# Second attention of a two-block transformer kernel: scores from stacked q_hi over q_lo in 128 array rows, weighted sum inside the gate unit

## The reference, cut to what matters

```python
q = rope(q_flat..., t); ks = rope(ks, t); kw = rope(kw, t)          # scaled by 64**-0.5
k_cmp = rope(compress_blocks(kc, ...), pos_c); v_cmp = compress_blocks(vc, ...)
p_cmp = masked_softmax(q @ k_cmp.T, pos_c <= t);  o_cmp = p_cmp @ v_cmp
p_sel = masked_softmax(q @ ks.T, causal);         o_sel = p_sel @ vs
p_win = masked_softmax(q @ kw.T, causal);         o_win = p_win @ vw
o = g[0] * o_cmp + g[1] * o_sel + g[2] * o_win    # g = sigmoid(gate_logits)
```

## Time and profile before

| | us |
|---|---|
| three timed runs | 1312.44, 1313.99, 1314.47; median 1313.99 |
| the profiled execution: its own time | 1314.33 |
| its span (first to last instruction) | 1312.3 |
| mean granted TensorE clock | 0.982 |
| PE busy | 1262.8 (96%) |
| DVE, ACT, POOL busy | 813.4, 589.7, 62.7 |

### The profile page before, as it was taken

One profiled execution on the slowest core, in us unless ns is written; L12 is line 12 of the kernel. 1 busy time (PEld: TensorE's weight loads), 2 busy tenths in 40 slices (PEclk: granted clock), 3 DMA queues, 4 the chain that ended last, 5 costly groups with the idle time before them and its releaser, 6 DMA issues.

```text
span 1312.3 us, 22759 instructions
## 1 busy us (share of the span) xinstructions
PE 1262.8 (96%) x8692; PEld 1138.8 (87%) x8692; DVE 813.4 (62%) x1294; ACT 589.7 (45%) x885; POOL 62.7 (5%) x72
## 2 busy tenths in 40 slices
PE   5899999999999999999998999998999999999997
PEld 3688888888886899889998999998898889999997
DVE  2677777753344755776675555655767767565664
ACT  2443234321233337544445556545445565544542
POOL 1000000000001000000001000002013102000001
PEclk9899999999999999999998999998899999999999
DMA  9544544453234244323453554544442224455542
GB/s 390 232 192 191 193 181 178 178 196 136 88 104 161 98 159 160 128 97 129 161 192 105 221 206 174 192 170 151 166 157 97 97 97 176 151 192 191 188 167 89
DMA packets 30957, 214.16 MB, mean 163 GB/s; under 512 B 3376, under 2 KB 4656, under 8 KB 5936
## 3 DMA queue, kind: packets, MB, share of 16 engines
q1 hardware_dynamic: 30032, 209.73, 43.4%
q10 hardware_dynamic: 864, 3.58, 0.7%
HBM read 212.24 MB, written 1.05 MB: 163 GB/s over the span
## 4 chain that ended last, share of the span: by engine, by line
PE 87%; DVE 5%; ACT 3%; DMA 3%; issue 1%; DVEq 0%; ACTq 0%; SPq 0%
PE ps_u L1510 26%; PE ps_u L1511 26%; PE ps_u L1512 26%; DMA raw<-in_stream 1%; PE ps_a L1457 1%; DMA scr<-in_mods 1%; PE ps_a L1446 1%; DVE w_lo L848 1%; ACT w_hi L486 1%; PE ps_a L1474 1%; DVE sq L925 1%; PE ps_a L1663 1%; PE ps_a L1648 1%; PE ps_a L1823 1%; PE ps_a L1463 1%
## 5 line engine op out<-in xcount | busy, mean ns | idle before, releaser
L1510 PE MATMUL ps_u<-x_hi,w_hi 128*128 128x256 f32 (+1 forms) x1744 | 544.3, 312 | 14.8 <-DVE x_lo L936 10.3
L1511 PE MATMUL ps_u<-x_lo,w_hi 128*128 128x256 f32 (+1 forms) x1744 | 537.8, 308 | 0.0
L1512 PE MATMUL ps_u<-x_hi,w_lo 128*128 128x256 f32 (+1 forms) x1744 | 537.4, 308 | 0.0
L848 DVE TENSOR_TENSOR w_lo<-raw,w_hi 128x1024 fp32r<-128x1024 f32 x322 | 393.9, 1227 | 210.7 <-ACT w_hi L486 209.0
L486 ACT ACTIVATE w_hi<-raw 128x1024 fp32r<-128x1024 f32 x322 | 338.2, 1056 | 285.1 <-PE ps_u L1512 247.1
L1510 PEld LDWEIGHTS ps_u<-x_hi,w_hi 128*128 128x128 f32 x1744 | 336.2, 193 | 39.6 <-issue 20.5
L1511 PEld LDWEIGHTS ps_u<-x_lo,w_hi 128*128 128x128 f32 x1744 | 336.5, 193 | 15.4 <-issue 0.5
L1512 PEld LDWEIGHTS ps_u<-x_hi,w_lo 128*128 128x128 f32 x1744 | 336.2, 193 | 15.2
L1510 PE MATMUL ps_u<-h_hi,w_hi 128*128 128x256 f32 (+1 forms) x800 | 246.0, 308 | 1.4 <-DVE h_lo L1426 1.4
L1511 PE MATMUL ps_u<-h_lo,w_hi 128*128 128x256 f32 (+1 forms) x800 | 245.1, 306 | 0.0
L1512 PE MATMUL ps_u<-h_hi,w_lo 128*128 128x256 f32 (+1 forms) x800 | 245.0, 306 | 0.0
(11 more groups left out here) (237 smaller groups left out, 823.0 us busy)
## 6 DMA issues: line engine op xcount, KB each, us to landing
raw<-in_stream SPq DMA_DIRECT2D x153, 1024.0 KB, 4.7
wide_scr<-in_mods SPq DMA_DIRECT2D x18, 1024.0 KB, 6.8
scr<-in_mods SPq DMA_DIRECT2D x18, 1024.0 KB, 7.2
raw<-in_stream SPq DMA_DIRECT2D x8, 768.0 KB, 4.1
x<-in_tokens ACTq DMA_DIRECT2D x2, 1024.0 KB, 14.1
wide_scr<-in_cmp_w SPq DMA_DIRECT2D x2, 1024.0 KB, 9.1
sq<-in_cmp_w SPq DMA_DIRECT2D x2, 1024.0 KB, 7.8
out<-x SPq DMA_DIRECT2D x4, 256.0 KB, 2.2
```

The costliest lines, as they stand in the source:

```text
L848: dve.tensor_tensor(w_lo[:, k % 2, cols], raw[:, k % 2, cols], w_hi[:, k % 2, cols].bitcast(F32), ALU.subtract).then_inc(l_ready, 1)
L1510: pe.matmul(dst, wh, xh, start=(kc == 0), stop=False)
L1511: pe.matmul(dst, wh, xl, start=False, stop=False)
L1512: ins = pe.matmul(dst, wl, xh, start=False, stop=(kc == span - 1))
```

## The change

The scores no longer use plain fp32 matmuls over 64 rows. ACT makes an fp32r copy of each rotated operand and DVE the rest (value minus copy). For the queries the copy lies in one half of the 128 partitions and the rest in the other (`q2_st`, in the unused half of `x_hi`); for the keys the copy lies in both halves (part 0) and the rest over the first half with zeros opposite (part 1; `k2_st` in `x_lo`, `kc_st` in `h_hi`). A score is then two fp32r matmuls over 128 rows. POOL no longer copies queries, and `pool_group(r)` no longer waits for scores. `weighted(h-1)` computes 128 output rows (both groups; one is read) and stands before the last two of the eight row blocks of gate unit h. PE's heads are written out, not looped.

```diff
+        q2_st = x_hi[:, :, S:NB]
+        kc_st = h_hi[:, 4, 0:2 * G2 * NCP].rearrange("p (a g c) -> p a g c", a=2, g=G2)
+        k2_st = x_lo[:, :, S:NB].rearrange("p (a g b) n -> p a g b n", a=2, g=G2)
 # POOL
             for r in range(4):
-                pool.wait_ge(rope2_done, 3 + r if r < 2 else 4 + r)
-                if r:
-                    pool.wait_ge(qk_done, HQ + 2 * r)
-                else:
-                    pool.wait_ge(hid_turned, 1)
+                if r == 0:
+                    pool.wait_ge(hid_done, 2)
                     pool.wait_ge(gt_ready, 1)
-                pool.tensor_copy(q_cur[:, 0, :], q2[:, r, :]).then_inc(qcur_ready, 1)
                 pool_group(r)
 # ACT
+            def keys_hi():
+                act.wait_ge(rope2_done, 2)
+                for g in range(G2):
+                    for half in range(2):
+                        act.activation(k2_st[half * DH:(half + 1) * DH, 0, g, :, :],
+                                       kk2[g * DH:(g + 1) * DH, :].rearrange("p (b n) -> p b n", b=2), ACT.Copy).then_inc(k2_hi, 1)
+            def cmp_keys_hi():
+                act.wait_ge(k2_zeroed, 1)
+                act.wait_ge(rope2_done, 5)
+                for g in range(G2):
+                    for half in range(2):
+                        act.activation(kc_st[half * DH:(half + 1) * DH, 0, g, 0:NC], kc_r[g * DH:(g + 1) * DH, 1, :], ACT.Copy)\
+                           .then_inc(k2_hi, 1)
+            def queries_hi(r):
+                act.wait_ge(rope2_done, 3 + r if r < 2 else 4 + r)
+                for g in range(G2):
+                    rows = slice(g * DH, (g + 1) * DH)
+                    act.activation(q2_st[rows, 2 * r + g, :], q2[rows, r, :], ACT.Copy).then_inc(q2_hi, 1)
...
+            keys_hi()
             splits(0, k + 7)
+            queries_hi(0)
+            cmp_keys_hi()
+            queries_hi(1)
             splits(0, k + 8)
...
             head(0, 0, 0, None, first=True)
+            for r in range(2, R2H):
+                queries_hi(r)
 # DVE: keys_lo(), cmp_keys_lo() wait for all of k2_hi of their kind, two subtractions each
+            def queries_lo(r):
+                dve.wait_ge(q2_hi, G2 * (r + 1))
+                for g in range(G2):
+                    rows, others = slice(g * DH, (g + 1) * DH), slice((1 - g) * DH, (2 - g) * DH)
+                    dve.tensor_tensor(q2_st[others, 2 * r + g, :], q2[rows, r, :], q2_st[rows, 2 * r + g, :].bitcast(F32), ALU.subtract)\
+                       .then_inc(q2_stacked, 1)
...
             queries(1)
+            for g in range(G2):
+                dve.memset(k2_st[(1 - g) * DH:(2 - g) * DH, 1, g, :, :].bitcast(F32), 0.0)
+            dve.memset(kc_st.bitcast(F32), 0.0).then_inc(k2_zeroed, 1)
+            keys_lo()
...
             rope2(4, kc_r[:, 0, :], ps_a[:, 1, 0:NC], cos2[:, last:S:CS], sin2[:, last:S:CS], kc_r[:, 1, :])
+            queries_lo(0)
+            cmp_keys_lo()
+            queries_lo(1)
             pool_in(1)
...
             head(0, 0, 0, None, first=True)
+            for r in range(2, R2H):
+                queries_lo(r)
 # PE
+            def scores(h, g, first=False):
+                pe.wait_ge(q2_stacked, h + 1)
+                if first:
+                    pe.wait_ge(k2_stacked, 2 * G2)
+                else:
                     pe.wait_ge(exp_done, 2 * HQ + h)
...
+                for a in range(2):
+                    pe.matmul(lo, q[0], k2_st[:, a, g, :, 0:P], start=(a == 0), stop=(a == 1))
                 for qt in range(TT):
+                    for a in range(2):
+                        pe.matmul(ps_a[:, 1, 2 * P + qt * 16:2 * P + qt * 16 + 16], q[qt], kc_st[:, a, g, :],
+                                  start=(a == 0), stop=(a == 1))
+                for a in range(2):
+                    ins = pe.matmul(hi, q[1], k2_st[:, a, g, :, :], start=(a == 0), stop=(a == 1))
+                ins.then_inc(qk_done, 1)
...
-                    pe.matmul(ps_a[rows, 2, 0:S], v2_tok[:, b, 0, rows], probs_t[:, 2 * b, :], start=(b == 0), stop=False)
+                    pe.matmul(ps_a[:, 2, 0:S], v2_tok[:, b, 0, :], probs_t[:, 2 * b, :], start=(b == 0), stop=False)
...
-                unit(r, FIRST["gates2"] + g, from_x(S))
-                weighted(h - 1, 1 - g)
+                def weighted_within(kc):
+                    if kc == KD - 2:
+                        weighted(h - 1)
+                unit(0, FIRST["gates2"] + h, from_x(S), ready=weighted_within)
```

More of the change, by code:

```diff
@@ L312, in program @@
         rope2_done = sem("rope2_done")
+        k2_zeroed = sem("k2_lo_zeroed")
+        k2_hi = sem("k2_hi_done")
+        k2_stacked = sem("k2_stacked")
+        q2_hi = sem("q2_hi_done")
+        q2_stacked = sem("q2_stacked")
         v2_turned = sem("v2_turned")
@@ L1785, in _ @@
             pe.wait_ge(rope2_done, 5)
[L1788 to L1792, removed]
-                    pe.wait_ge(exp_done, 2 * HQ + h)
-                q = [q_cur[rows, 0, qt * P:(qt + 1) * P] for qt in range(TT)]
-                own = kk2[rows, :].rearrange("p (b n) -> p b n", b=2)[:, :, 0:P]
-                pe.matmul(ps_a[:, 1, 0:2 * P].rearrange("p (b n) -> p b n", b=2), q[0], own, start=True, stop=True)
-                for qt in range(TT):
-                    pe.matmul(ps_a[:, 1, 2 * P + qt * 16:2 * P + qt * 16 + NC], q[qt], kc_r[rows, 1, :], start=True, stop=True)
-                pe.matmul(ps_a[:, 0, :], q[1], kk2[rows, :], start=True, stop=True).then_inc(qk_done, 1)
+            def scores(h, g, first=False):
[3 more added lines that the diff above has]
+                else:
+                    pe.wait_ge(exp_done, 2 * HQ + h)
+                q = [q2_st[:, h, qt * P:(qt + 1) * P] for qt in range(TT)]
+                lo = ps_a[:, 1, 0:2 * P].rearrange("p (b n) -> p b n", b=2)
+                hi = ps_a[:, 0, :].rearrange("p (b n) -> p b n", b=2)
+                for a in range(2):
+                    pe.matmul(lo, q[0], k2_st[:, a, g, :, 0:P], start=(a == 0), stop=(a == 1))
+                for qt in range(TT):
+                    for a in range(2):
[4 more added lines that the diff above has]
+                ins.then_inc(qk_done, 1)
             def turns(h, first=False):
@@ L1815, in turns, with weighted @@
                 ins.then_inc(t_done, 1)
-            def weighted(h, g):
-                rows = slice(g * DH, (g + 1) * DH)
+            def weighted(h):
                 pe.wait_ge(pta_ready, HQ + h + 1)
@@ L1822, in weighted, with head @@
                 for b in range(2):
[L1823 to L1840 removed]
+                    pe.matmul(ps_a[:, 2, 0:S], v2_tok[:, b, 0, :], probs_t[:, 2 * b, :], start=(b == 0), stop=False)
+                    pe.matmul(ps_a[:, 2, P:S], v2_tok[:, b, 1, :], probs_t[:, 2 * b + 1, P:S], start=False, stop=False)
+                pe.matmul(ps_a[:, 2, 0:S], vc_tok[:].rearrange("p g d -> p (g d)"), q_cur[:, 1, :], start=False, stop=True)\
+                  .then_inc(pv_done, 1)
+            def head(h, g, second=False):
+                scores(h, g)
+                turns(h - 1, second)
+                def weighted_within(kc):
+                    if kc == KD - 2:
+                        weighted(h - 1)
+                unit(0, FIRST["gates2"] + h, from_x(S), ready=weighted_within)
+            scores(0, 0, first=True)
+            unit(0, FIRST["gates2"], from_x(S))
+            for h in range(1, H2):
+                head(h, h % 2, second=(h == 1))
             def mix(i):
@@ L1852, in _ @@
             mix(3)
-            weighted(7, 1)
+            weighted(7)
             def rows_done(kc):
```

22 lines of the change are left out of this document (11 added, 11 removed).

## The result

The changed kernel takes 1318.53 us (median of 13 runs, 1315.82 to 1321.05) against 1313.99 for the kernel before (13 runs, 1312.44 to 1316.08): ratio 1.003, 95% interval 1.0021 to 1.0039. Its profiled execution took 1316.72 us, span 1314.9, mean granted clock 0.980 (before: 1314.33, 1312.3, 0.982). The forecast was 1321.3 with 1314.5 to 1325.0.

What follows compares the result with a forecast made beforehand. PE, busy 96% of the span, was taken as the bound. Late start +6.0, six head periods +0.5 and tail +0.8 gave +7.3 us on the profiled 1314.33, so 1321.6, or 1321.3 for the median; range 1314.5 to 1325.

Steps and rivals of the forecast that it cites:

- the start of the heads: DVE, ACT and POOL work before the first heads: scores(2) comes later by 6.0 us, the largest term.
- PE's saving in the heads: PE, per head: 0.85 us less score work, waited away at the turns, leaving each head 0.09 us worse.
- Scores: PE's scores per head: 1.08 us (bounds 0.7 to 1.2) against 1.93 before.
- the rival of stacking that is no faster: Scores on PE: 128-row fp32r no quicker than 64-row fp32, period 10.8, total 1322; chance within the forecast's 0.64.
- Handover: Between gate unit and turns: PE waits for head_lo, turns start 1.88 us after the unit, 0.7 us waited per head.
- The head period that I named as a sign: PE's time from head to head: 10.6 to 10.7 us would show the forecast right, under 10.2 wrong.
- A head without its wait: PE's work in one head with no waiting: 9.94 us, 0.63 less than before.
- Six periods and the tail: From scores(2) to behind gate unit 7: +0.5 us for six periods, +0.8 for the wait of turns(7).
- The queue before the split: DVE before maxima(0): 0.25 us for keys, 0.3 for POOL, 2.65 waiting for ACT's copies and half split.
- POOL beneath DVE: POOL's back-to-back windows slow DVE's rotations: 0.3 us before the compressed keys, 0.8 for queries r = 2 and 3.
- Sum at scores(2): Start of the third head's scores on PE: +6.0 us in all, +5.3 with the clock held.
- The clock: PE after 5 us idle before scores(1): granted clock falls to half speed, 1.9 us lost before weighted(0).

Runs made afterwards that it cites:

- e9: Changed kernel with POOL's windows waiting for heads again, rotations of query pairs 2 and 3 behind maxima(0), small copies spread between split halves and heads; ratio 1.0001 to before.
- e8: Changed kernel with head_hi (ACT) and head_lo (DVE) moved ahead of half 0 of the split; ratio interval 0.9985 to 1.0003 to the kernel before.
- e6: Changed kernel with the weighted sum still inside the gate unit but in 64 output rows instead of 128; ratio 1.0043 to the kernel before.
- e2: Changed kernel with POOL's windows 1 to 3 waiting for the scores of heads 1, 3 and 5 again; 1.3 us less by the ratios.
- e12: e10 with POOL's windows back to back, as in the changed kernel; ratio interval 0.9969 to 0.9987 to the kernel before.
- e10: Changed kernel with the edits of e8 and e9 together; 1309.88 us, 0.27% under the kernel before.
- e1: Changed kernel with head_hi ahead of gates_out on ACT and head_lo ahead of the tick on DVE; ratio 1.0012 to the kernel before.
- e13: Changed kernel with 22 extra fp32r matmuls, results unread, filling PE's wait for exps(0); no total time given, scores(2) at 74.22 us behind the gate logits.
- e4: Changed kernel with stacked scores kept and the weighted sum back behind the gate unit in 64 rows; no total time given, mean head period 10.11 us.
- e3: Changed kernel with DVE's rotations of query pairs 2 and 3 moved from before maxima(0) to behind it; 0.4 us less by the ratios.
- e11: e9 with the weighted sum back behind the gate unit in 64 rows, as in e4; 1312.32 us.

## Why the prediction was right, and where its terms were off

**Direction and cause.** Right: the loss is the start of the heads (e9 gives most of it back), and PE's saving in the heads is mostly waited away (e8 gives it back). The total came as close as it did in part because two misses of opposite sign met: the start cost 0.9 more than its term, the heads 2.2 less.

**Scores.** Predicted 1.08 with a step of 0.08; e8 shows 1.16 from scores to turns. Right, and the rival of stacking that is no faster falls. Rows of fp32r with 16 columns run at 0.09 each (four from 1012.95 to 1013.31), as taken.

**Handover.** Predicted: turns at U + 1.88, 0.7 of wait a head. Measured: 1.65 to 2.27 over seven heads, 4.4 us of wait in seven. Right, and e8 shows the cause: with the order alone changed, the wait is gone. The head period that I named as a sign, 10.6 to 10.7, did not come (10.37 on average), for the reason in the next paragraph. What I missed is DVE's half split in front of head_lo, which makes it up to 0.4 later than the chain through ACT (h_hi is done at 1003.21, h_lo begins at 1003.76).

**A head without its wait.** Predicted 9.94, measured 9.52 (e8). This is the term that was mis-sized. In e8 the turns take 0.80 (1015.50 to 1016.30), where I had 0.85. I took every step into or out of fp32 as 0.08 dearer. The step into the wide sum is the plain 0.12 (the narrow one of e6 enters at 0.21), so 0.08 drops out there; the step behind the turns is still 0.20, as taken. The largest part is the sum with its step out: 1.74, where I had 1.93 + 0.08, so 0.27. Together that is 0.40 of the 0.42. Six periods and the tail, predicted +1.3, came to -0.86 (turns(7) minus scores(2): 63.69 against 64.55). The Trainium skill (TensorE: Matmul & The Clock Gate, section LDWEIGHTS) has a weight load grow with its columns; the widened sum would be 0.5 us dearer by it if loads were bare, an estimate. Here the widened sum is 0.24 cheaper than the narrow one of e6 (1.74 against 1.98), so no such price shows; what the loads cost by themselves is not shown.

**The queue before the split.** Predicted 0.25 + 0.3 + 2.65 = 3.2, measured 4.1 at DVE's own split. It has two parts. The compressed keys' rotation ended 1.0 later than before (975.16 - 928.58 = 46.58 against 45.57), where I had 0.25 + 0.3. From there to DVE's split it took 3.08, where I had 2.65 for ACT's small copies and its half of the split. I had DVE's six subtractions hide in ACT's queue, and they do, by a little: with POOL beneath they run from 975.18 to 978.07, and the split behind them still waits 0.16 for ACT; in e2, where they are shorter, it waits 0.28 and comes 3.09 behind the rotation all the same. So ACT's chain is the term that was too small here. What the subtractions do delay is the low half of the compressed keys, which stands behind query pair 0 in DVE's list (976.41 to 977.10): scores(0) waits 1.7 us for it and comes 1.73 later, where I had 0.5.

**POOL beneath DVE.** Predicted 1.1 on maxima(0) (0.3 and 0.8), measured 1.1 (e2) and 0.8 at scores(2). Right for the changed kernel, though 0.2 of it fell before the split and 0.9 behind it, and one trace with overlapping intervals carries it. With nothing else to cover it, the trace of e12 puts turns(0) 2.2 later than e10's. The Trainium skill (SBUF — State Buffer, section SBUF: two separate sides) names DVE operations with two SBUF inputs and those in a 2-port perf mode. In this case it was not only the TENSOR_TENSORs that were stretched: four TENSOR_SCALARs on one tile with a column of factors went from 1.01 us to 1.95 and 2.28. In which mode they ran, no trace here shows.

**Sum at scores(2).** Predicted +6.0, measured +6.89; maxima(0) predicted +4.0, measured +5.01. Scores(1) waited 3.1 and not 5: scores(0) came 1.2 later than I had it, and gate unit 0 ran in part at half clock, so PE arrived 3 us later. Exps(0) released scores(1) 4.28 behind maxima(0), where I had 4.19.

**The clock.** The fall came, from 988.3 to 995.1, and an earlier one that I did not have. I had 1.9 us lost at PE, of which 0.7 reach scores(2). In the trace of the changed kernel nothing of it arrives, as worked out here. PE's timeline:

```profile
998.49 0.28 PE L1573 MATMUL ps_u<-x_hi,w_lo 128*128 128x256 f32 x1
998.81 0.67 PE L1890 MATMUL ps_a<-scr 128*128 128x256 f32 x2
```

PE would have been ready for weighted(0) at 998.49 + 0.12 = 998.61, and DVE's copy that it reads ended at 998.66: two chains of equal length, and a faster clock alone would have gained nothing there. The term was not wrong for good, and that it came to nothing is in part luck: where the fall came later or lasted longer, PE was the later of the two. From turns(0) to weighted(0) PE needs 5.2 us at full clock (1015.50 to 1020.69 in e8, one head); it took 7.7 in e1 and e13 and 7.3 in e12, and weighted(0) came 0.9, 0.9 and 1.3 us behind its copy, against 0.15 here. So the price was between nothing and 1.2 us, by where the fall lay. No run holds the clock, so what that would bring stays unmeasured.

**Total.** At the merge the terms say +5.6 against my +7.3: +0.9 at the start, -2.2 in the heads and their tail, -0.4 from turns(7) on.

**What stays open.** The medians put the changed kernel +4.5 above before (3.9 by the ratio), and all edits but e10 likewise come out 0.7 to 2.4 us better against before by their ratios than at the merge. Part of it is that the single profiled execution of the kernel before took 245.4 us from the merge to the end, the longest of all. That stretch varies between 244.1 and 245.4 without a pattern that I could tie to the edits, and the start of the gate logits between 928 and 931.3. Why the clock falls behind scores(0)'s 1.7 us wait in some of the kernels and not in others is open too, and so is what the new places of the small copies in e9 bring by themselves.

## What to carry to other kernels

When work leaves the bounding engine, ask what stood behind that work: here 3.8 us of matmuls covered a chain of three instructions through two other engines, and moving the last two of them up in their lists brought 4.7 us by the ratios, as much as the whole edit had lost. Work added before the first use of a pipeline can hold up all that follows; with part of it placed between the heads, e9 got back 4.8 of the 6.9 us. Judge such a change from one common point in both traces, part by part; the total alone hid a loss of 6.9 and a gain of 1.3.

## What the runs showed of the hardware that I had not expected

- A change of number format alone does not always cost PE a step, and neither does a change of the array's tile. Into the sum, from fp32r to fp32: 0.12 us at 128\*128 (changed kernel), 0.20 and 0.21 at 128\*64 (before, e6). From the turns into the unit, fp32 to fp32r, both 128\*128: 0.20 in both kernels. From a unit into the gate logits, fp32r both, 128\*128 to 128\*24: 0.12, in PE's timeline of the kernel before:

```profile
930.17 0.28 PE L1512 MATMUL ps_u<-x_hi,w_lo 128*128 128x256 f32 x1
930.29 0.28 PE L1712 MATMUL ps_a<-x_hi,wg_hi 128*24 128x256 f32 x1
```

- A matmul set with 128 output rows beat the same with 64: 1.74 against 1.98 for ten instructions of fp32.
- With 1.7 us of wait before scores(0), the granted clock fell to 1.2 GHz for 3 to 4 us in the changed kernel, e4, e6 and e8, and did not in e1, e3, e12 and e13 with the same wait. Behind or within the waits of scores(1) or turns(0) it fell in the changed kernel and in every edit, in e9 to e11 with no longer wait there than 2.2 us. 2.8 us of filler, with 2.0 and 1.5 us idle behind it, did not hold it (e13).
- Four TENSOR_SCALAR on DVE of 128x128 last 1.01 us alone, 1.49 to 2.28 with POOL beneath.
